# Turning three of four column blocks of a gated mix with VectorE transposes and DMAs in place of TensorE, in a two-layer encoder on one core

## What is computed

```python
def layer(x, ...):
    h = rms_norm(x, pre_g)
    parts = _split(h @ w_in, WIDTHS)            # queries, keys, values, gates
    oa, ob = attention_1(...), attention_2(...) # 8 heads of 128 each
    mix = jnp.concatenate([oa.reshape(b, s, -1) * jax.nn.silu(ga),
                           ob.reshape(b, s, -1) * jax.nn.silu(gb)], axis=-1)
    return x + rms_norm(mix @ w_out, post_g)
```

## Time and profile before

| | |
|---|---|
| median of 3 runs | 1184.09 us (1183.4 to 1186.24) |
| profiled execution, its own time | 1184.91 us |
| its span | 1183.1 us |
| TensorE busy | 1164.0 us, 98% |
| VectorE busy | 721.6 us, 61% |
| ScalarE busy | 579.7 us, 49% |
| mean granted TensorE clock | 0.998 |
| weight loads on SP | 195 of 1024 KB, median 5.0 us from issue to landing |
| moved by DMA | 244.18 MB |

### The profile page before, as it was taken

The page is one execution under the profiler, slowest core; times in us unless marked ns, Lnnn a source line. Parts: engine busy times, 40 slices in busy tenths (PEclk is TensorE's granted clock), DMA queues, the critical chain, the costliest instruction groups (busy, mean ns, idle before and its releaser), DMA issues.

```text
span 1183.1 us, 14592 instructions
## 1 busy us (share of the span) xinstructions
PE 1164.0 (98%) x5492; PEld 971.4 (82%) x5492; DVE 721.6 (61%) x837; ACT 579.7 (49%) x756; POOL 93.0 (8%) x129
## 2 busy tenths in 40 slices
PE   7999999999999999999999999999999999999997
PEld 5777888888888888788888888888888888888886
DVE  5376556656665955764656555565746567658554
ACT  6545445544555644564545454444444444445442
POOL 2400002000000000010000101102011002000000
PEclk9999999999999999999999999999999999999999
DMA  9987766744646555455767666666766666454541
GB/s 365 260 235 278 226 224 210 231 174 147 244 153 243 178 198 194 145 211 177 237 218 227 220 205 224 211 220 204 239 200 191 228 205 212 144 205 149 202 150 72
DMA packets 77224, 244.18 MB, mean 206 GB/s; under 512 B 26048, under 2 KB 42560, under 8 KB 51696
## 3 DMA queue, kind: packets, MB, share of 16 engines
q1 hardware_dynamic: 74448, 233.87, 58.4%
q0 software_dynamic: 1856, 7.38, 2.4%
q10 hardware_dynamic: 864, 2.18, 0.5%
HBM read 223.47 MB, written 8.39 MB: 196 GB/s over the span
## 4 chain that ended last, share of the span: by engine, by line
PE 91%; DMA 4%; DVE 1%; ACT 1%; SPq 1%; issue 1%; ACTq 0%; DVEq 0%
PE acc L451 84%; PE bank_x L591 2%; DMA raw<-weights 2%; DMA probs<-x_nat 2%; PE bank_y L544 1%; SPq L319 1%; ACT w_hi L699 1%; PE bank_y L533 1%; PE bank_x L587 1%; PE bank_x L575 1%; PE bank_y L560 0%; PE bank_x L560 0%; PE bank_y L540 0%; PE bank_x L488 0%; PE bank_y L488 0%
## 5 line engine op out<-in xcount | busy, mean ns | idle before, releaser
L451 PE MATMUL acc<-w_hi,act_hi 128*128 128x512 f32 x1560 | 616.1, 395 | 2.3 <-DVE w_lo L979 2.0
L451 PE MATMUL acc<-w_lo,act_hi 128*128 128x512 f32 x1560 | 608.1, 390 | 0.0
L979 DVE TENSOR_TENSOR w_lo<-raw,w_hi 128x2048 fp32r<-128x2048 f32 x195 | 450.1, 2310 | 192.6 <-ACT w_hi L699 192.3
L699 ACT ACTIVATE w_hi<-raw 128x2048 fp32r<-128x2048 f32 x195 | 373.5, 1916 | 298.5 <-PE acc L451 273.4
L451 PE MATMUL acc<-w_hi,act_lo 128*128 128x512 f32 x1560 | 417.7, 389 | 0.0
L451 PEld LDWEIGHTS acc<-w_hi,act_lo 128*128 128x128 f32 x1560 | 292.7, 188 | 62.2 <-DVE act_lo L988 0.4
L451 PEld LDWEIGHTS acc<-w_hi,act_hi 128*128 128x128 f32 x1560 | 293.2, 188 | 61.4 <-DVE w_lo L979 3.9
L451 PEld LDWEIGHTS acc<-w_lo,act_hi 128*128 128x128 f32 x1560 | 293.3, 188 | 56.9
L706 ACT ACTIVATE unit<-acc,pre_r 128x512 f32<-128x512 f32 x78 | 49.3, 684 | 114.8 <-PE acc L451 114.4
L396 POOL TENSOR_TENSOR rope_c<-unit,cst 128x256 f32<-128x256 f32 (+1 forms) x19 | 14.1, 742 | 791.7 <-ACT unit L706 658.9
L721 ACT ACTIVATE probs<-scores,negm 128x256 f32<-128x256 f32 (+1 forms) x80 | 36.4, 458 | 31.0 <-DVE negm L1067 25.3
(11 more groups left out here) (168 smaller groups left out, 591.1 us busy)
## 6 DMA issues: line engine op xcount, KB each, us to landing
raw<-weights SPq DMA_DIRECT2D x195, 1024.0 KB, 5.0
qk_raw<-postg SPq DMA_DIRECT2D x176, 64.0 KB, 2.1
p_moved<-p_blocks SPq DMA_DIRECT2D x16, 256.0 KB, 5.5
probs<-p_moved SPq DMA_DIRECT2D x64, 64.0 KB, 2.0
resid<-x_turned SPq DMA_DIRECT2D x8, 256.0 KB, 9.2
mix<-rpb POOLq DMA_DIRECT2D x32, 64.0 KB, 23.7
postg<-post_g POOLq DMA_DIRECT2D x2, 1024.0 KB, 8.5
resid<-x_perm POOLq DMA_DIRECT2D x2, 1024.0 KB, 8.0
```

Source lines behind the costliest of these rows:

```text
L451: m = nc.tensor.matmul(tiles[t][:, :], a[:, kt, t * P:(t + 1) * P], w[:, buf, kk * NB:(kk + 1) * NB], start=(kt == 0 and a is act_hi and w ...
L699: nc.scalar.activation(w_hi[:, at % SPLIT, :], raw[:, at % RAW, :], ACT.Copy).then_inc(S["hi_ready"], 1)
L979: nc.vector.tensor_tensor(w_lo[:, at % SPLIT, :], raw[:, at % RAW, :], w_hi[:, at % SPLIT, :].bitcast(F32), ALU.subtract).then_inc(S["lo_r ...
```

## The change

Of the four column blocks of the mix TensorE turns only block 0, in slot 2. Blocks 1 to 3 are turned in the way of the gathers. Behind the gate of the block VectorE transposes its 32x32 blocks into the new buffer `mix_blocks` (`turn_mix_blocks`, two operations of 128x512). SP moves them with 16 DMAs of 32 KB into `mix_raw`, which has two halves used in turn (`move_mix`, in its slots 2, 4 and 6, ahead of that slot's load). ScalarE and VectorE split from there in slots 5, 7 and 9 (`mix_hi`, `mix_lo`). In layer 0 a move's destination rows are cut into pieces of 32 elements, and the split reads them in the other order of tokens, in four operations; in layer 1 the rows are whole and the split is one operation. `mix_blocks` is a single buffer: from the second block on VectorE waits for `mix_in`, the landing of the move before, ahead of its transposes. The two new buffers take no room of their own: they lie over the buffers of the queries and keys, which the tail does not use. The sequence of the output's chunks becomes (0,0) (1,0) (0,1) (1,1) (0,2) (1,2) (0,3) (1,3), then blocks 2 and 3, and the weights are packed in it.

```diff
-OUT_ORDER = ([(0, c) for c in range(3)] + [(1, c) for c in range(3)] + [(0, 3), (1, 3)]
-             + [(2, c) for c in range(4)] + [(3, c) for c in range(4)])
+OUT_ORDER = [(n, c) for c in range(4) for n in range(2)] + [(n, c) for n in (2, 3) for c in range(4)]
-TURN_SLOTS = (2, 4, 5, 7)
+TURN_SLOT = 2
+MOVE_SLOTS = (2, 4, 6)
+SPLIT_SLOTS = (5, 7, 9)
+MOVE_DMAS = 16 * QUADS * QUADS
...
+            def move_mix(layer, c):                                   # SP
+                sp.wait_ge(S["mix_turned"], 3 * layer + c)
+                for a in range(QUADS):
+                    for q in range(QUADS):
+                        rows = slice(q * QUAD, (q + 1) * QUAD)
+                        dst = raw_by_tile[rows, c % 2, :, :, a, :] if layer == 0 else mix_raw[rows, c % 2, a, :, :, :]
+                        sp.dma_start(dst, mix_blocks[a * QUAD:(a + 1) * QUAD, q, :, :, :]).then_inc(S["mix_in"], 16)
...
                 for s in range(CHUNKS + len(OUT_ORDER)):
+                    if s in MOVE_SLOTS:
+                        move_mix(layer, MOVE_SLOTS.index(s) + 1)
                     load(CHUNK0[layer] + BODY * BODIES[layer] + s + 2 + RAW)
...
-                        if half == 0 and s in TURN_SLOTS:              # TensorE
-                            k = TURN_SLOTS.index(s)
-                            if k == 0:
-                                pe.wait_ge(S["o_taken"], CREDIT + HEADS[layer])
-                            turn_mix(layer, k, 0)
-                            turn_mix(layer, k, 1)
+                        if half == 0 and s == TURN_SLOT:
+                            pe.wait_ge(S["o_taken"], CREDIT + HEADS[layer])
+                            turn_mix(layer, 0)
+                            turn_mix(layer, 1)
...
+            def mix_hi(layer, c):                                     # ScalarE
+                act.wait_ge(S["mix_in"], MOVE_DMAS * (3 * layer + c))
+                if layer == 0:
+                    for k in range(CK):
+                        src, dst = in_token_order(c, act_hi, k)
+                        m = nc.scalar.activation(dst, src, ACT.Copy)
+                else:
+                    m = nc.scalar.activation(in_rows(c, act_hi), raw_rows(c), ACT.Copy)
+                m.then_inc(S["turn_hi"], 2)
...
+            def turn_mix_blocks(layer, c):                            # VectorE
+                dve.wait_ge(S["gate_done"], CHUNKS * layer + c + 1)
+                if layer or c > 1:
+                    dve.wait_ge(S["mix_in"], MOVE_DMAS * (3 * layer + c - 1))
+                for t in range(NT):
+                    m = nc.vector.transpose(mix_blocks[:, :, :, t, :],
+                                            mix[:, t, c * NB:(c + 1) * NB].rearrange("p (k q n) -> p q k n", q=QUADS, n=QUAD))
+                m.then_inc(S["mix_turned"], 1)
+            def mix_lo(layer, c):
+                dve.wait_ge(S["turn_hi"], 16 * layer + 10 + 2 * c)
+                ...
+                m.then_inc(S["turn_taken"], 2)
...
+                    if s in SPLIT_SLOTS:                               # VectorE; ScalarE likewise with mix_hi
+                        mix_lo(layer, SPLIT_SLOTS.index(s) + 1)
                     if s in GATE_SLOTS:
-                        gate(layer, GATE_SLOTS.index(s))
+                        c = GATE_SLOTS.index(s)
+                        gate(layer, c)
+                        if c > 0:
+                            turn_mix_blocks(layer, c)
                     if s < CHUNKS + len(OUT_ORDER):
                         split_lo(g0 + s + 2)
```

More of the change, by code:

```diff
@@ L159, in build @@
         sb("q_room", [P, NT * UH, P], F32R)
+        with nc.sbuf_tensor("mix_blocks", [P, QUADS, CK, NT, QUAD], F32) as mix_blocks:
+            pass
         k_hi = sb("k_hi", [P, QUADS, NT * UH * QUAD], F32R)
         with nc.sbuf_tensor("qk_raw", [P, QUADS, 2, NT * UH * QUAD], F32) as qk_raw:
+            pass
+        with nc.sbuf_tensor("mix_raw", [P, 2, QUADS, CK, NT, QUAD], F32) as mix_raw:
             pass
@@ L220, in build @@
         bias_a = resid[:, :, :].rearrange("p t n -> p (t n)")
+        raw_by_tile = mix_raw[:, :, :, :, :, :].rearrange("p s a k t n -> p s (a k t n)").rearrange(
+            "p s (k t a n) -> p s k t a n", k=CK, t=NT, n=QUAD)
         scores_flat = scores[:, :, :].rearrange("p a n -> p (a n)")
@@ L233, in build @@
                  "nat_in first_in first_hi first_lo hi_ready lo_ready chunk_used tile_done proj_ready roped rope_a "
-                 "turn_full turn_hi turn_taken qk_turned qk_in qk_hi qk_ready k_full k_split k_ready g_ready "
+                 "mix_turned mix_in turn_full turn_hi turn_taken qk_turned qk_in qk_hi qk_ready k_full k_split k_ready g_ready "
                  "s_full masked maxed negm_ready probs_ready sink_ready "
@@ L278, in turned_next, with raw_rows, in_rows, in_token_order @@
             return None if u is not None and (u.kind == "D" or layer == 0 and at == end) else at
+        def raw_rows(c):
+            return mix_raw[:, c % 2, :, :, :, :].rearrange("p a k t n -> p (k t) a n")
+        def in_rows(c, dst):
+            return dst[:, c * CK:(c + 1) * CK, :].rearrange("p k (t a n) -> p (k t) a n", t=NT, n=QUAD)
+        def in_token_order(c, dst, k):
+            src = raw_by_tile[:, c % 2, k, :, :, :].rearrange("p t a (h b n) -> p n b (t a h)", h=2, b=4)
+            return src, dst[:, c * CK + k, :].rearrange("p (n b r) -> p n b r", n=4, b=4)
         def split_units(u):
@@ L496, in turn_x, with turn_mix @@
                 turn(16 + k, [resid[:, t, kt * P:(kt + 1) * P] for kt in range(c * CK, (c + 1) * CK)])
[L498 to L502, removed]
+            def turn_mix(layer, k):
+                if k == 0:
+                    pe.wait_ge(S["gate_done"], 4 * layer + 1)
                 turn(16 * layer + 8 + k,
@@ L815, in turned @@
                     return
-                act.wait_ge(S["turn_full"], f + 1 - 8)
+                act.wait_ge(S["turn_full"], f - 7 - (6 if f >= 16 else 0))
                 if 16 <= f < 24:
@@ L937, in _ @@
                         out_root(0)
[L938 to L941, removed]
+                    if s == TURN_SLOT:
+                        turned(16 * layer + 8, layer)
+                        turned(16 * layer + 9, layer)
+                    if s in SPLIT_SLOTS:
+                        mix_hi(layer, SPLIT_SLOTS.index(s) + 1)
                     if s in GATE_SLOTS:
@@ L1237, in gate @@
                 m.then_inc(S["gate_done"], 1)
+            def turn_mix_blocks(layer, c):
[8 more added lines that the diff above has]
+                dve.wait_ge(S["turn_hi"], 16 * layer + 10 + 2 * c)
+                if layer == 0:
+                    for k in range(CK):
+                        (src, hi), (_, lo) = (in_token_order(c, dst, k) for dst in (act_hi, act_lo))
+                        m = nc.vector.tensor_tensor(lo, src, hi.bitcast(F32), ALU.subtract)
+                else:
+                    m = nc.vector.tensor_tensor(in_rows(c, act_lo), raw_rows(c), in_rows(c, act_hi).bitcast(F32), ALU.subtract)
+                m.then_inc(S["turn_taken"], 2)
             def scale_out(layer, n, t):
```

## The result

The changed kernel takes 1202.76 us (median of 4 runs, 1200.3 to 1204.68) against 1184.83 (4 runs, 1183.4 to 1186.24): the ratio is 1.0145, 95% interval 1.0129 to 1.0162. It is 17.9 us slower; 1205 was forecast, in a range of 1194 to 1221. The profiled execution took 1200.3 us (span 1198.5), 15.4 more than that of the kernel before; it is the fastest of the four. A ratio in this document can differ a little from the quotient of the two medians (1.0151 here); the interval covers both.

What follows compares the result with a forecast made beforehand. TensorE, busy 98% of the span, was taken as the bound. The terms 0.7 + 13.8 + 2.7 + 4.9 + 4.0 - 5.2 = +20.9 us on 1184.09 gave 1205 us, own range 1199 to 1213.

Steps and rivals of the forecast that it cites:

- six pairs of turns gone: TensorE, three blocks in two layers: turns at 0.87 us a pair removed, 5.2 us saved.
- transposes ahead of chunk 3, layer 0: VectorE's 1.4 us of transposes delay the split against 0.7 us of slack, so TensorE waits 0.7 us.
- stall at chunk 5, layer 0: TensorE waits 6.9 us: the split, queued behind VectorE's buffer wait, is ready at 17.8 against 10.9.
- from there to chunk 7, beyond 10.9 us: Second stall, as move 2 waits for the same things: 6.9 us in layer 0, 4.9 us in layer 1.
- stall at chunk 5, layer 1: TensorE waits 2.7 us: the split is ready at 1094.3, TensorE would be there at 1091.6.
- restarts behind chunk 7: TensorE's clock returns slowly after each layer's second stall: 2.0 us twice, 4.0 us; 0 if it stays up.
- D: Time from a move's start to its landing: 13.5 us in layer 0, 11.5 us in layer 1.
- packet's price: Layer 0's moves: 30 ns per packet, 256 packets of 128 bytes per DMA engine, 7.7 us of each.
- a first landing gap under 7 us: Sign that the prediction is wrong, beside issue at 0.44 us or under, or stalls at chunks 6, 8 or 10.
- Rival A: SP's moves are issued faster, 0.44 us each: 1197 us, or 1185 if layer 0 gains too; chance 0.20.
- rival C: Packets of 128 bytes are dear, D 21 us in layer 0: +42, 1226 us; chance 0.17 including cases between.
- Rival B: Buffer wait over before VectorE gets to it, D under 6.5 us: faster, 1180 us; chance 0.05.

Runs made afterwards that it cites:

- E8: Changed kernel with two halves of mix_blocks, eight of 16 issues on GpSimd's queue, blocks transposed behind their slot's split: 1180.69 us against 1185.78, ratio 0.9959.
- E1: Changed kernel with two halves of mix_blocks in place of the single buffer: 1188.85 us against 1185.88 for the kernel before, ratio 1.0019.
- E5: Changed kernel, single buffer, each block transposed behind its slot's split, blocks 2 and 3 a slot later: 1190.66 us against 1185.78, ratio 1.0038.
- E2: Changed kernel, single buffer, eight of each move's 16 DMAs issued by GpSimd's queue: 1185.85 us against 1185.88 for the kernel before, ratio 0.9996.
- E6: Changed kernel with each move cut into 32 DMAs of 16 KB: 1263.91 us against 1185.78 for the kernel before, ratio 1.0653.
- E3: Kernel before with only the new sequence of the output's chunks: 1185.34 us against 1185.88, ratio 0.9995.
- E7: Changed kernel with layer 0's moves in whole 1 KB rows, split in one operation, token reordering left out: 1200.87 us against 1185.78, ratio 1.0137.

## Why the prediction was right

By its own steps, with what the profiled execution of the changed kernel shows:

| step | forecast | measured |
|---|---|---|
| six pairs of turns gone | -5.2 | -5.1 (E8 against before; 3.2 to 6.4 by its interval) |
| transposes ahead of chunk 3, layer 0 | 0.7 | 0.8 |
| stall at chunk 5, layer 0 | 6.9 | 6.0 |
| from there to chunk 7, beyond 10.9 us | 6.9 | 16.02 - 10.9 = 5.1, 1.5 of it slow restart |
| stall at chunk 5, layer 1 | 2.7 | 2.3 |
| from there to chunk 7, beyond 10.9 us | 4.9 | 16.23 - 10.9 = 5.3, 1.7 of it slow restart |
| restarts behind chunk 7 | 4.0 | 1.7 in layer 0, 0.1 in layer 1 |
| sum | +20.9 | 0.8 + 6.0 + 5.1 + 2.3 + 5.3 + 1.8 - 5.1 = +16.2 |

The profiled execution is 15.4 us longer than that of before, the medians differ by 17.9. The first line is taken from another kernel (E8), so the sum is an account and not a measurement of its own; what makes the other three executions longer than the profiled one is not shown by any trace.

**The mechanism** was as forecast: which engine waits, for what, what stands behind it, and at which chunks TensorE pays. E1 shows that the cost hangs on the single buffer, E5 that it hangs on the place of the wait in VectorE's queue, E2 and E6 that a move's length follows its serial issue. The neutral parts, the sequence of chunks (E3) and the splits, cost nothing that could be told from the noise; the load issued behind a move, some 10 us late, did not hold up anybody.

**Two terms were too large**, 2.7 and 2.2 us; the small ones on the other side bring the whole to the 4.7 by which the sum was over. One is layer 0's two stalls. D, the length of a move, was taken as 13.5 us, with every weight and packet time added up ahead of the landing. It was 13.0 and 12.1, which makes 1.9 of the 2.7 us; the rest are the steps around it, in each stall 0.4 us from the split to the first issue in place of 0.6, and 3.5 us for transposes and split in place of 3.7. The packet's price was the wrong figure. The 30 ns came from a window of loads from HBM with a part of a weight load in it, in which 0.20 MB in 584 packets make 342 bytes on average, not 256; here a packet of 128 bytes took 12.4 ns. By that the packets are 3.2 us of each engine and not 7.7, an estimate; the same working then gives 5.0 + 3.2 - 0.6 + 1.4 = 9.0 us, less than the issue's 12.1, and the packets pass while SP is still issuing. E7 puts what is left of them at about 0.6 us per move. The lower end of the estimate, the gathers' 12.1 us, would have been the better choice. The other is the restart behind the second stall: 2.0 us twice. Layer 0 paid 1.7 and layer 1 nothing: its clock stayed up through 3.6 us of idle time. That a restart costs 1.5 to 1.7 us where the clock does fall was nearly right; that it falls each time was not. On the other side, the second stall of layer 1 was 0.4 us larger than forecast: its move took 12.4 us in place of 11.5, with 10.97 us of issue where the one before took 10.01.

Two details of the prediction do not hold by its own working. The lower end of its own range, 1199, comes out at 1198.2 with D = 12.1 and no restarts. And "a first landing gap under 7 us" was named as a sign of being wrong: as VectorE's wait it would be met (6.43 us) by a mechanism that was right, and the list of what should be seen allows that wait 4 to 11 us; only read as the length of the move (13.0 us) does the sign tell anything.

Rival A (issues at 0.44 us) is out: the median issue of a move is 0.596 us, at half the gathers' bytes. Of the two rules beside rival C in the Trainium skill's "DMA: Bandwidth & Descriptors", that of the section Why small descriptors are slow (HBM only), by which transfers within SBUF are spared the price of small descriptors, is nearer to what E7 shows (0.6 us per move) than that of the Specifications. Rival B asked for a wait that is over before VectorE gets there, by a fast issue; E8 gets that by the second buffer and the second queue, and its 1180.69 us is B's 1180.

Open is why some moves have one issue that takes 1.5 us or more (1.67 at 401.19 and 1.55 at 1105.58 in the changed kernel); both fall 2 to 6 us behind the issue of the weight load ahead, but no run set that apart.

## What to carry to other kernels

When work is taken off the busiest engine and given to a chain of other engines, the price is in the waits it adds: for each new wait, name the engine it stands on, what is queued behind it, and when that is due. A wait for a buffer (the reader's end, not the data) is easily missed; here the waits cost some 23 us (17.9 + 5.1) to save 5, and putting them behind one or two splits gave back 13. Count the issues of small DMAs, not only their bytes (here 0.6 us each), and try them on two queues.

## What was not expected of the hardware

Reading SBUF in strides of 64 bytes was slower than reading PSUM with the same pattern. ScalarE's split of 128x256 took 0.632 us (0.402 or less from PSUM), VectorE's 0.606 (0.41). In layer 1, with runs of 32 elements, 128x1024 took 1.06 and 1.22 us, as a plain operation does. Here are the instructions on `mix_raw` of the changed kernel: minimum, median and maximum in ns.

```profile
L869 ACT ACTIVATE act_hi<-mix_raw x12: 618/632/652, 408.8 to 442.2; 128x256 fp32r<-128x256 f32 x12
L1295 DVE TENSOR_TENSOR act_lo<-mix_raw,act_hi x12: 580/606/619, 414.5 to 444.4; 128x256 fp32r<-128x256 f32 x12
L871 ACT ACTIVATE act_hi<-mix_raw x3: 1057/1060/1061, 1100.5 to 1132.2; 128x1024 fp32r<-128x1024 f32 x3
```

It cost nothing in time here, since both engines had room in those slots.

The clock did not follow the length of a stall. Of the changed kernel in layer 1: after the shorter stall (2.3 us, ending at 1104.14) the granted clock fell to 0.50 while TensorE was at work again. After the longer one (3.6 us, ending at 1120.37) it did not fall. Busy time by stretch, clock third from the end:

```profile
1104.00:1106.00 2.00, 1.86 (x6) 1.51 (x7) 2.00 (x1) 0.31 (x1) 0.00 (x0) 0.71 0.46 78
1106.00:1108.00 2.00, 2.00 (x7) 1.52 (x6) 2.00 (x3) 0.00 (x0) 0.00 (x0) 0.50 0.95 389
1118.00:1120.00 2.00, 0.00 (x0) 0.00 (x0) 2.00 (x2) 1.59 (x1) 0.00 (x0) 1.00 0.82 332
1120.00:1122.00 2.00, 1.63 (x7) 1.40 (x8) 2.00 (x2) 0.00 (x0) 0.00 (x0) 1.00 0.50 74
```
